# One inference step on one core: two modulation vectors ahead of the recurrent layer and three inside it, input matrix in chunks of 256 columns, gate projections three blocks late

## The reference, cut to what matters

```
mp = jnp.split(cond_ctx @ mod_w[layer] + mod_b[layer], N_MOD, axis=-1)
ms = jnp.split(cond_lat @ mod_w[layer] + mod_b[layer], N_MOD, axis=-1)
...
gate, u = jnp.split(xn @ w_in, 2, axis=-1)
u = _centred_dwconv(u, conv_w, conv_b).astype(F32)
a_f, b_f = _rglru_coeffs(u, w_a[0], b_a[0], w_x[0], b_x[0], lam[0])
h_f = _linear_scan(a_f, b_f, h0_f.astype(F32))
...
h = h_f + jnp.flip(h_b, 1)
y = (h * jax.nn.gelu(gate.astype(F32))).astype(xn.dtype) @ w_out
```

## Time and profile before

| | us |
|---|---|
| median of 3 runs (2082.1 to 2083.9) | 2083.8 |
| profiled execution | 2084.6 |
| its span, first to last instruction | 2082.8 |
| TensorE busy in the span | 1812.0 |
| VectorE busy | 1544.0 |
| ScalarE busy | 1214.7 |
| POOL busy | 570.5 |

### The profile page before, as it was taken

One profiled execution on the slowest core, in us unless ns is written; L12 is line 12 of the kernel. 1 busy time (PEld: TensorE's weight loads), 2 busy tenths in 40 slices (PEclk: granted clock), 3 DMA queues, 4 the chain that ended last, 5 costly groups with the idle time before them and its releaser, 6 DMA issues.

```text
span 2082.8 us, 26307 instructions
## 1 busy us (share of the span) xinstructions
PE 1812.0 (87%) x8919; PEld 1265.4 (61%) x8919; DVE 1544.0 (74%) x1822; ACT 1214.7 (58%) x1518; POOL 570.5 (27%) x320
## 2 busy tenths in 40 slices
PE   1599969789999999999568789898699999999996
PEld 0388847656666666666357578777366666666664
DVE  0457663479999999999346376634699999999994
ACT  0356751168777777777241145522378777777774
POOL 0122230103434444342200050000223434434331
PEclk7699979599999999999779779997799999999997
DMA  9400271799999999999760330006399999999992
GB/s 342 137 1 1 83 292 48 299 339 366 361 375 358 378 359 378 362 378 365 189 134 0 128 121 1 1 1 269 135 361 376 359 378 359 376 357 378 365 376 83
DMA packets 139904, 519.04 MB, mean 249 GB/s; under 512 B 14944, under 2 KB 15232, under 8 KB 138815
## 3 DMA queue, kind: packets, MB, share of 16 engines
q1 hardware_dynamic: 124288, 484.22, 60.4%
q0 software_dynamic: 7216, 24.79, 6.2%
q10 hardware_dynamic: 8334, 9.17, 1.4%
HBM read 496.90 MB, written 21.24 MB: 249 GB/s over the span
## 4 chain that ended last, share of the span: by engine, by line
PE 55%; DVE 19%; issue 13%; ACT 5%; DMA 4%; ACTq 2%; POOL 1%; DVEq 0%; SPq 0%; POOLq 0%
PE ps L729 19%; PE ps L733 10%; DVE whl L1482 9%; PE ps L687 5%; PE ps L931 4%; PE ps L978 2%; ACT whl L1099 2%; DVE W L1513 2%; DMA ring<-in_at_w_qkv 2%; ACTq L1188 2%; PE ps L951 2%; PE ps L967 1%; PE ps L667 1%; PE ps L761 1%; DVE W L1500 1%
## 5 line engine op out<-in xcount | busy, mean ns | idle before, releaser
L1482 DVE TENSOR_TENSOR whl<-ring,whl 128x1024 fp32r<-128x1024 f32 x768 | 970.0, 1302 | 79.3 <-ACT whl L1099 66.7
L1099 ACT ACTIVATE whl<-ring 128x1024 fp32r<-128x1024 f32 x768 | 805.5, 1059 | 253.1 <-PE ps L733 234.9
L729 PE MATMUL ps<-whl,xs_hl 128*80 128x512 f32 x2048 | 561.0, 396 | 7.3 <-DVE xs_hl L1506 3.8
L729 PEld LDWEIGHTS ps<-whl,xs_hl 128*80 128x80 f32 x2048 | 298.7, 149 | 169.4 <-issue 6.2
L733 PE MATMUL ps<-whl,xs_hl 128*80 128x512 f32 x1024 | 323.3, 397 | 10.8 <-DVE whl L1482 7.5
L729 PE MATMUL ps<-whl,hs_hl 128*80 128x512 f32 x1024 | 280.9, 396 | 3.4 <-ACT hs_hl L1008 3.4
L532 POOL TENSOR_TENSOR W<-W 80x1024 f32<-80x1024 f32 x32 | 100.0, 3125 | 486.4 <-ACT W L1137 486.4
L733 PEld LDWEIGHTS ps<-whl,xs_hl 128*80 128x80 f32 x1024 | 147.6, 149 | 112.8 <-DVE whl L1482 37.9
L729 PEld LDWEIGHTS ps<-whl,hs_hl 128*80 128x80 f32 x1024 | 153.4, 150 | 89.3 <-ACT hs_hl L1008 3.8
L733 PE MATMUL ps<-whl,hs_hl 128*80 128x512 f32 x512 | 160.8, 396 | 0.0
L527 POOL COPY si<-idx_t 80x1 uint32 (+1 forms) x32 | 128.2, 4007 | 0.0
(11 more groups left out here) (253 smaller groups left out, 2508.7 us busy)
## 6 DMA issues: line engine op xcount, KB each, us to landing
ring<-in_moe_w_gate SPq DMA_DIRECT2D x128, 1024.0 KB, 6.7
ring<-in_moe_w_up SPq DMA_DIRECT2D x128, 1024.0 KB, 6.7
ring<-in_moe_w_down SPq DMA_DIRECT2D x128, 1024.0 KB, 6.1
ring<-in_mod_w SPq DMA_DIRECT2D x48, 1024.0 KB, 8.5
ring<-in_rg_w_in SPq DMA_DIRECT2D x8, 1024.0 KB, 15.0
ring<-in_at_w_qkv SPq DMA_DIRECT2D x8, 768.0 KB, 23.3
x_hat<-r ACTq DMA_DIRECT2D x2, 2560.0 KB, 18.9
ring<-in_rg_w_out SPq DMA_DIRECT2D x4, 1024.0 KB, 10.2
```

The lines of the kernel that those rows point to most:

```text
L729: nc.tensor.matmul(ps[0:CE, bank + n, :], xhl[:, part, k, :], w[:, 0, n * 512:(n + 1) * 512], start=(k == 0 and part == 0), stop=False)
L1099: nc.scalar.activation(whl[:, q % HL, 0, :], ring[:, slot, (q % 2) * D:(q % 2 + 1) * D], ACT.Copy).then_inc(whi_ok, 1)
L1482: v.tensor_tensor(whl[:, q % HL, 1, :], ring[:, n % MSLOTS, (q % 2) * D:(q % 2 + 1) * D], whl[:, q % HL, 0, :].bitcast(F32), ALU.subtract) ...
```

## The change

SP issues x first, then vectors 0 and 1, then the input matrix in eight chunks of 256 columns (two blocks of u or of g each), in the order in which the loop uses them, with vectors 2, 3, 4 between. The `bd` and router loads move to POOL's queue, behind the landing of x. Only vectors 0 and 1 stand ahead of the layer; 2, 3 and 4 are multiplied at the end of blocks 1, 3 and 5 of the loop and turned in the block after. The g projection of block b stands in iteration b + 3 (`LAG`). The columns go through two buffers and three PSUM banks in the order `COLUMNS`: u0 u1 u2 u3 g0 u4 g1 u5 g2 u6 g3 u7 g4 g5 g6 g7. VectorE's scans of block c stand in iteration c + 2, its product with gelu in c + 4. The output weights are split by POOL in iterations 7 to 10 (high and low part of the first six, the high part of the last two); VectorE takes two. On the way into layer 1 SP reads `x_mid`, and the gains are read once per partition and spread by POOL.

```diff
+MOD_SLOT = (0, 4, 4, 4, 4, 8, 0, 4, 8, 0, 4, 8)
...
+LAG = 3
+COLUMNS = []
+for _b in range(KB + LAG):
+    COLUMNS += [("u", _b)] * (_b < KB) + [("g", _b - LAG)] * (_b >= LAG)
+CHUNK_SLOT = {"u": (0, 1, 3, 1), "g": (2, 0, 2, 3)}
+RG_MODS = {1: 2, 3: 3, 5: 4}
...
-            sp.wait_ge(rows_in, 16 * 11)
+            sp.dma_start(tok(r2), x_tiles).then_inc(x_in, 16)
             load_mod(0)
             load_mod(1)
-            load_mod(2)
-            for s in range(KB):
-                load(s, ring[:, s, :], rg_w_in[s * P:(s + 1) * P, :], (ring_used, used(s // 4, s % 4)))
-            load_mod(3, (wcol_lo_ok, lambda s: 2 * KB))
-            load_mod(4, (wcol_lo_ok, lambda s: 2 * KB))
+            for kind, c in (("u", 0), ("u", 1), ("g", 0), ("u", 2)):
+                load_columns(kind, c, (ring_used, used(0, CHUNK_SLOT[kind][c])))
+            load_mod(2, (ring_used, lambda s: used(1, s)))
+            load_columns("g", 1, split("u", 1))
+            load_mod(3, (ring_used, lambda s: used(2, s)))
+            load_columns("u", 3, split("u", 3))
+            load_mod(4, (ring_used, lambda s: used(3, s)))
+            load_columns("g", 2, split("g", 1))
+            load_columns("g", 3, split("u", 5))
...
-            sp.wait_ge(x_mid_in, 16)
+            sp.wait_ge(scattered, 16 * NE)
+            sp.dma_start(tok(r2), x_mid.rearrange("(t p) d -> p t d", p=P)).then_inc(x_mid_in, 16)
...
+            pool.wait_ge(consts, 2)
+            pool.wait_ge(x_in, 16)
+            for m, w in enumerate((rg_w_a[0], rg_w_a[1], rg_w_x[0], rg_w_x[1])):
+                for h in range(2):
+                    pool.dma_start(bd[h * RB:(h + 1) * RB, m, :, h * RB:(h + 1) * RB],
+                                   w.rearrange("(c h) i j -> h i c j", h=2)[h]).then_inc(bd_in, 16)
...
+            for b in range(KB + LAG):
+                if 0 < b < KB:
+                    column_high(column("u", b) + 1)
+                if b >= LAG and b - LAG < KB - 1:
+                    column_high(column("g", b - LAG) + 1)
+                if 1 <= b <= KB:
...
+                for k in range(2 * (b - KB + 1), 2 * (b - KB + 2)) if b >= KB - 1 else ():
+                    out_weight(k, k < 6)
...
-            pool.dma_start(gains[:, 0:NH * HD].rearrange("p (h n) -> p h n", n=HD),
-                              at_q_norm.unsqueeze(1).to_broadcast([P, NH, HD])).then_inc(small_in, 16)
+            pool.dma_start(raw_gains[:, 0, :], at_q_norm.to_broadcast([P, HD])).then_inc(small_in, 16)
...
+            for b in range(KB + LAG):
+                if b < KB:
+                    project("u", b)
+                if b - 1 in RG_MODS:
+                    turn_row(RG_MODS[b - 1])
+                if 1 <= b <= KB:
...
+                if b >= LAG:
+                    project("g", b - LAG)
+                if b in RG_MODS:
+
+                    pe.wait_ge(sig_ok, 8 * b)
+                    cond_product(RG_MODS[b])
...
             eng.wait_ge(consts, 4)
-            for b in range(KB + 1):
+            for b in range(KB + LAG):
+                if 0 < b < KB:
+                    column_rest(column("u", b) + 1)
+                elif b >= KB and column("g", b - LAG) + 1 < len(COLUMNS):
+                    column_rest(column("g", b - LAG) + 1)
+                if b > LAG:
+                    gated(b - LAG - 1)
+                if 2 <= b < KB + 2:
+                    scans(b - 2)
+                if b == KB + 2:
+                    mixed_rest(0, range(3))
                 if b < KB:
```

More of the change, by code:

```diff
@@ L140, in mod_bank @@
         def mod_bank(n):
[L142 removed]
+            return 6
         def mod_rows(n):
@@ L272, in runs, with column, chunk, column_bank @@
             return out
+        def column(kind, b):
+            return COLUMNS.index((kind, b))
+        def chunk(kind, b):
+            return ring[:, CHUNK_SLOT[kind][b // 2], :].rearrange("p (k n) -> p k n", k=KB)[:, :, b % 2 * P:(b % 2 + 1) * P]
+        def column_bank(kind, b, h):
+            p = 2 * column(kind, b) + h
+            return p % 3 if p >= 2 else 4 + h
+        def turn_bank(n):
+            return 3 if n in RG_MODS.values() else 2
+        def out_bank(t):
+            return 2 * ((t + 1) % 2)
         def used(v, s):
@@ L428, in _, with column_high @@
             pool.wait_ge(vec_ok, 1)
-            for v in range(3):
+            for v in range(2):
                 mod_bias(v)
+            def column_high(i):
+                kind, b = COLUMNS[i]
+                if i >= 2:
+                    before, b2 = COLUMNS[i - 2]
+                    pool.wait_ge(u_mm if before == "u" else g_mm, b2 + 1)
+                if b % 2 == 0:
+                    slot = CHUNK_SLOT[kind][b // 2]
+                    pool.wait_ge(slot_ready[slot], ready("in" if (kind, b // 2) in (("u", 0), ("u", 1), ("g", 0), ("u", 2)) else "in2", slot))
+                nc.gpsimd.tensor_copy(wcol[i % 2][:, 0], chunk(kind, b)).then_inc(wcol_hi_ok, 1)
@@ new lines, in conv @@
+            def conv(b):
+                uc = ucs[b % 2]
+                eng.wait_ge(u_ok, 3 * (b + 1))
+                if b >= 2:
+                    eng.wait_ge(z_mm, b - 1)
+                    eng.wait_ge(iu_ok, 2 * (b - 1))
+                step(v.tensor_scalar(uc, upad[:, 0:UC], vec[:, b, R_CW:R_CW + 1], vec[:, b, R_CB:R_CB + 1], ALU.mult, ALU.add))
+                for k in range(1, 4):
+                    ins = v.scalar_tensor_tensor(out=uc, in0=upad[:, k:k + UC], scalar=vec[:, b, R_CW + k:R_CW + k + 1],
+                                                 in1=uc, op0=ALU.mult, op1=ALU.add)
+                    if k < 3:
+                        step(ins)
+                ins.then_inc(conv_ok, 1)
```

406 lines of the change are left out of this document (203 added, 203 removed).

## The result

The changed kernel takes 2034.1 us (median of 4 executions, 2032.9 to 2038.8), where the kernel before takes 2083.8: a ratio of 0.976, with a 95% interval of 0.975 to 0.978. It is faster by 49.7 us; 66.8 were forecast. The profiled execution of after is the longest of its four: its span is 2037.0 us, 45.8 less than the span before.

What follows compares the result with a forecast made beforehand. Taken as bounds: the opening with TensorE mostly idle, the recurrent loop with its tail, and the way into layer 1. From 2084.6, minus 52.3 (opening, loop, tail) and 15 (layer 1), 2017.3, so 2017 us; range 2000 to 2040.

Steps and rivals of the forecast that it cites:

- Opening, 46.9 forecast: Up to the first projection: reordered loads start the turns at 42.7 and the projection at 53.5, where 100.4 was.
- I take 3: Opening: small loads ahead of the second vector cost 3 us (3 by bytes, 4.6 by packets), so it lands at 35.5.
- 1 KB packets, 2.7 us a chunk: Opening: each 1 MB input-matrix chunk takes 2.7 us by bytes; upper bound 10.9 if 1 KB packets cost like 4 KB.
- Rival D: Input-matrix chunks take 10.9 us, vector 2 lands at 90 and its product stands 14.5 us: 2032; chance 0.08.
- Rival A: Opening: POOL is held by its new load queue as ScalarE was, +13 us: 2030; chance 0.07.
- Loop: Recurrent loop: TensorE's work plus waits of 3.5, 1.5 and 1.5 sum to 151.8 us, so z7 ends at 205.3.
- Rival C: Loop: VectorE and POOL together bound it, some 0.8 us a block: 2023; chance 0.06.
- Rival E: Loop: new gaps drop TensorE to the low clock and it stays there, 113 us more: 2130; chance 0.03.
- Tail: From z7's end to the output product's second tile: POOL's weight splits add waits; second tile at 260, where 312.3 was.
- The hold of 9 us by the first pair: Tail: POOL's first two output-weight splits delay g6's column, so block 7's sigmoids start at 214, nine after z7.
- The clash: Tail: two POOL subtractions beside VectorE's last scans and gate product slow them by 4.0 us (0 to 8).
- Into layer 1, 15 forecast: Before layer 1's qkv: ScalarE's 16.2 us wait for weights goes, less about 1 for small loads: 15 us (8 to 17).

Runs made afterwards that it cites:

- e1: Kernel after, with GpSimd issuing the eight bd and two router loads only after its first two weight-column casts; 2029.9 us.
- e2: Kernel after, with the same ten small loads in SP's queue between the first and second modulation vector; nothing won, median not given in the text.
- e5: Kernel after, with the third modulation vector's product moved from block 1 to 3 and the fourth's from 3 to 4; time the rival's (2032 to 2034).
- e3: Kernel after, with GpSimd's six output-weight subtractions cut to 8 of 1024 columns, low parts left out of the result; 2022.7 us.
- e10: Kernel after, with all eight output-weight subtractions on VectorE and GpSimd only casting; 2026.5 us.
- e12: Kernel before, with only layer 1's gain vectors read in 256 pieces, x_mid still by GpSimd and the weights behind it on SP; 2066.6 us.
- e8: Kernel after, with layer 1's gain vectors read as before in 2560 pieces; 66.0 us from x_mid read to first qkv product (after: 37.7).
- e4: Kernel after, with GpSimd's casts of g6's and g7's columns put ahead of output-weight pairs, nothing left out; 2037.3 us.

## Why the prediction was right, and where its sizes were off

**What bounds the kernel** held: all three places gave time, the experts none.

**Opening, 46.9 forecast, 41.4 measured.** The step that failed is the price of the small loads, "I take 3" for 1.2 MB. The forecast had the second vector in at 32.5 without them; in e1, where they come later, it was in at 32.1. With them it was in at 41.4, where 35.5 was forecast. So they cost 9 us, and 8.8 to 9.2 at the first projection. They also were not "all in front of" the second vector: the first one's last half was held as well (31.4 for 21.5). The product of the second vector ran at the low level, 32 matmuls in 7.22 us where the earlier trace rows has 3.66, but it ended 1.9 us behind the last landing, as forecast, so that cost nothing here. The rest was right: 4.8 us from there to the turns (5.2 forecast) and 10.9 on to the first projection (10.8). The mistake was to read 12 ns from queue 10's row: those were packets of 64 bytes in step with large ones, and 4096 of the 6144 pieces have 256 bytes, which took 22 ns in e2. Even at 12 ns the sum was 4.6, and 3 was taken.

**1 KB packets, 2.7 us a chunk:** nearly right, 3.0 us a chunk at the 350 GB/s of 45 to 50 us. Rival D falls: TensorE waited for no load inside the loop. Rival A falls too: GpSimd's queue was free at 20.2.

**Loop.** The waits were named right: 3.5 us at block 1's product, 3.3 in two waits for gelus (15.5 less the tail's 12.2; 3.0 forecast). From the start of z3 to that of z5, 140.2 to 185.1, the terms add up to 44.6 and the trace has 44.9. The step that failed is the sum's first three blocks: z7 ends at 221.3, 16 us late, 5.5 from the opening and 10.5 from the loop, nearly all of it ahead of z3. The rows give 2.9 for block 1's product (6.6 us for 3.7), 1.8 for z1, 1.3 for u4 and 0.8 for u0, in stretches whose mean clock is 0.67 to 0.96, and 3.2 for a wait that was not in the list: u4 for its column, whose subtraction stood behind the convolution on VectorE. About 2 of all this are this execution's own (e5 above). e5 moved the product and won 1.4 to 2.6 us; that fits a chain of ScalarE and VectorE that is longer than TensorE's work while there is no gate projection to do. Rival C had VectorE right and the place wrong: the loop as a whole is not bound there. Rival E exists in small, as stretches at the low level that cost some 7 us.

**Tail.** The hold of 9 us by the first pair is there: 8.3 (ScalarE's wait), and e3 and e10 show that GpSimd's subtractions make 4.4 of it. The second hold was in the sum too. The clash was mis-sized, 4.0 for 7.4: VectorE's eight instructions from 246.0 to 261.4 are that much longer than elsewhere. By the rule of the Trainium skill (SBUF — State Buffer, "SBUF: two separate sides") both subtractions count in full, 6.0, which is nearer than my half. Of the tail's 4.5 us (280.5 for 260, less the 16 of z7) some 2 are there when VectorE has done its last part for the first tile, at 272.0 for 254. The other 2.5 are a step that failed by itself, "the first seven eighths of the tile lie under these waits": the tile could start only with VectorE's first low part, at 264.0, and from there to the second tile it is 16.5 us of TensorE's work, as the 16.1 before.

**Into layer 1, 15 forecast, 12 measured.** The wait for the weights is gone as forecast, but "less about 1 for small loads that now share the engines" was 4: `x_mid` landed after 14.6 us instead of 10.1, and ScalarE was at the weights 34.5 us after the read's issue instead of 30.4. And the gain was put down to two edits together; e12 and e8 show that the new gain loads gave all of it and the order of the queues took some away.

**Sum.** 67.3 less 5.5 (opening), 10.5 (loop), 4.5 (tail) and 3 (way into layer 1) are the 44 that the first qkv product shows. The spans differ by 45.8, the medians by 49.7; the last 4 us are in the spread of what follows the first qkv product and were not traced further. The sign "qkv's first product at 1055" was on the time scale of before and had the last gain alone; on that of the other signs it is 1071.4 - 67.3 = 1004, and the trace has 1027.3.

That 2034 lies between 2000 and 2040 is in part luck. The forecast's own bounds, +3, +4 and +7, end at 2031; the loop's sum, the largest error, had no bound at all, and the upper end of the range came from the times of rivals A, C and D, none of which held as stated.

## What to carry to other kernels

Count the pieces of a load and not only its bytes, take their price from rows of the same load, and ask which large load they will run beside: here 6144 small pieces cost some 9 us, in GpSimd's queue as in SP's, and 2560 of another load cost 17. Moving a large load in front of them only put it among them (e8). Work that is moved to GpSimd beside a busy VectorE is paid twice, as a hold when it stands in front and as a clash when it stands beside; a subtraction of 2.4 to 3.5 us there was cheaper as one of 1.2 to 2.1 us on VectorE. And a lag that hides a chain behind other work leaves the first blocks without that work: walk them one by one, with the low clock that can follow a gap, before the steady block is multiplied.

## What the runs showed of the hardware that was not expected

- Small pieces share the 16 engines of all queues: with 6368 of them in 19 us the rate fell from 407 to 285 GB/s, 22 ns for a piece of at most 256 bytes. In e8 the 2560 pieces of the gain vectors (256 bytes each), at an estimated 190 ns each, held `x_mid`, 2.6 MB in another engine's queue, for 42.8 us.
- VectorE's scans clash with GpSimd's subtractions like its multiplications: 3.32 us for 1.28 in e4. A GpSimd cast beside such an instruction stretches it too: 2.05 for 1.22 at 236.9 in e10.
- SP was held by its own ten small loads for 21 us in e2 (5.2 to 26.0), as ScalarE was in the kernel before, while GpSimd issued the same ten between 12.6 and 20.2 in after.
